# The lower part of the down weights moved from GpSimd to VectorE in two feed-forward stages

## What is computed

```
def _swiglu(h, w_gate, w_up, w_down):
    return (jax.nn.silu(h @ w_gate) * (h @ w_up)) @ w_down
...
g = lax.ragged_dot(xs, w_gate, group_sizes)
u = lax.ragged_dot(xs, w_up, group_sizes)
y = lax.ragged_dot(jax.nn.silu(g) * u, w_down, group_sizes)
```

## Time and profile before

| | |
|---|---|
| median of 3 runs | 4415.4 us (4410.6 to 4421.4) |
| the profiled execution | 4412.7 us, of which the span of the trace is 4410.9 us |
| TensorE matmul busy | 3861.9 us, 88% of the span |
| VectorE busy | 2323.4 us, 53% |
| ScalarE busy | 1755.2 us, 40% |
| GpSimd busy | 826.3 us, 19% |
| dense stage, about | 740 to 1520 us |
| expert stage, about | 1750 to 4380 us |

### The profile page before, as it was taken

The page is one execution under the profiler, slowest core; times in us unless marked ns, Lnnn a source line. Parts: engine busy times, 40 slices in busy tenths (PEclk is TensorE's granted clock), DMA queues, the critical chain, the costliest instruction groups (busy, mean ns, idle before and its releaser), DMA issues. The chain is left out here.

```text
span 4410.9 us, 65249 instructions
## 1 busy us (share of the span) xinstructions
PE 3861.9 (88%) x23414; PEld 3521.9 (80%) x23415; DVE 2323.4 (53%) x3372; ACT 1755.2 (40%) x2324; POOL 826.3 (19%) x319
## 2 busy tenths in 40 slices
PE   5998867999999762698999989988899998998993
PEld 3974445877877651688999989988899998998993
DVE  2338733454545452586654444448654487544555
ACT  5146613322322131555443333335533355443443
POOL 0000001111111121332222122213221233222222
PEclk8989878999999986899999999999999999999997
DMA  5136634323332233675553434346544366444554
GB/s 169 38 125 240 229 94 172 105 95 95 105 95 86 78 132 90 201 232 183 185 169 133 143 132 149 126 144 231 196 144 143 129 219 210 156 149 146 175 167 186
DMA packets 433192, 661.23 MB, mean 150 GB/s; under 512 B 33361, under 2 KB 348881, under 8 KB 432977
## 3 DMA queue, kind: packets, MB, share of 16 engines
q1 hardware_dynamic: 413026, 587.84, 40.0%
q0 software_dynamic: 15776, 55.61, 3.6%
q10 hardware_dynamic: 4176, 15.21, 0.9%
HBM read 599.32 MB, written 59.29 MB: 149 GB/s over the span
## 5 line engine op out<-in xcount | busy, mean ns | idle before, releaser
L1847 POOL TENSOR_TENSOR moe_d_lo<-moe_raw_d,moe_d_hi 128x2048 fp32r<-128x2048 f32 x126 | 582.8, 4625 | 1823.0 <-ACT moe_d_hi L1985 1823.0
L2153 DVE SCALAR_TENSOR_TENSOR moe_y_t<-moe_y,moe_cols,moe_y_t 128x256 f32<-128x256 f32 (+3 forms) x936 | 482.2, 534 | 185.5 <-PE moe_y L1898 176.9
L1896 PE MATMUL moe_g<-moe_x,moe_g_hi 128*128 128x352 f32 (+3 forms) x1344 | 421.2, 313 | 36.6 <-issue 36.3
L2100 DVE TENSOR_TENSOR moe_g_lo<-moe_raw_g,moe_g_hi 128x2048 fp32r<-128x2048 f32 x127 | 360.9, 2842 | 135.6 <-ACT moe_g_hi L1985 134.3
L1897 PE MATMUL moe_g<-moe_x,moe_g_hi 128*128 128x352 f32 (+3 forms) x1344 | 420.6, 313 | 0.0
L1896 PE MATMUL moe_y<-moe_h,moe_d_hi 128*128 128x352 f32 (+3 forms) x1344 | 417.9, 311 | 2.1 <-DVE moe_y_t L2153 1.1
L1898 PE MATMUL moe_g<-moe_x,moe_g_lo 128*128 128x352 f32 (+3 forms) x1344 | 419.2, 312 | 0.0
L1897 PE MATMUL moe_u<-moe_x,moe_u_hi 128*128 128x352 f32 (+3 forms) x1344 | 416.1, 310 | 0.0
L1897 PE MATMUL moe_y<-moe_h,moe_d_hi 128*128 128x352 f32 (+3 forms) x1344 | 416.0, 310 | 0.0
L1896 PE MATMUL moe_u<-moe_x,moe_u_hi 128*128 128x352 f32 (+3 forms) x1344 | 415.3, 309 | 0.0
L1898 PE MATMUL moe_u<-moe_x,moe_u_lo 128*128 128x352 f32 (+3 forms) x1344 | 415.0, 309 | 0.0
(11 more groups left out here) (317 smaller groups left out, 9504.4 us busy)
## 6 DMA issues: line engine op xcount, KB each, us to landing
moe_raw_g<-in_moe_w_gate SPq DMA_DIRECT2D x127, 1024.0 KB, 5.6
moe_raw_u<-in_moe_w_up SPq DMA_DIRECT2D x127, 1024.0 KB, 5.0
moe_raw_d<-in_moe_w_down SPq DMA_DIRECT2D x126, 1024.0 KB, 4.9
att_w_mod<-in_w_ada SPq DMA_DIRECT2D x20, 2048.0 KB, 8.5
scratch_y<-att_zeros SPq DMA_DIRECT2D x11, 2048.0 KB, 13.8
ffn_raw_g<-in_ffn_w_gate SPq DMA_DIRECT2D x22, 1024.0 KB, 5.4
ffn_raw_u<-in_ffn_w_up SPq DMA_DIRECT2D x22, 1024.0 KB, 5.4
ffn_raw_d<-in_ffn_w_down SPq DMA_DIRECT2D x22, 1024.0 KB, 4.8
```

The costliest lines, as they stand in the source:

```text
L1847: pool.tensor_tensor(d_lo[par][:, :, :], raw_d[:, :, :], d_hi[par][:, :, :].bitcast(F), ALU.subtract)\
L1896: pe.matmul(bank[:, 0:width], wh, moving[:, 0, 0:width], start=start, stop=False)
L2100: dve.tensor_tensor(lo[par][:, :, :], raw[:, :, :], hi[par][:, :, :].bitcast(F), ALU.subtract).then_inc(split, 1)
L2153: dve.scalar_tensor_tensor(y_t[:, db, 0:cols], y_ps[db % 4][:, 0:cols], gate, y_t[:, db, 0:cols], ALU.mult, ALU.add).then_inc(y_added, 1)
```

## The change

The subtraction that gives `d_lo` is taken off GpSimd's program and put into VectorE's step, after the add of block 4 (in a step without adds, after the rest of hidden f=1). The first increment of `d_split` moves with it. GpSimd keeps only the fetching of tokens.

```diff
         def _(pool):
             pool.sem_inc(x_turned, X0)
 
-            def rest_d(p, c, par):
-
-                n = p * C + c
-                pool.wait_ge(d_rounded, n + 1)
-                pool.tensor_tensor(d_lo[par][:, :, :], raw_d[:, :, :], d_hi[par][:, :, :].bitcast(F), ALU.subtract)\
-                    .then_inc(d_split, 1)
-
...
             def one_pass(p):
                 if has_next(p):
                     fetch(p + 1)
-                chunk_pairs(pool, p, 0, C - 1, lambda c, par: rest_d(p, c, par))
-
-            pool.sem_inc(d_split, W0)
+
...
             dve.sem_inc(u_split, W0)
+            dve.sem_inc(d_split, W0)
...
+            def rest_d(p, c, par):
+                rest(p * C + c, par, raw_d, d_hi, d_lo, d_rounded, d_split)
...
                     rest_hidden(p, c, par, 1, width)
                     if share:
-                        for db in range(2, KD):
+                        for db in range(2, 5):
+                            add(p, c - 1, db, cols, share == 1)
+                    rest_d(p, c, par)
+                    if share:
+                        for db in range(5, KD):
                             add(p, c - 1, db, cols, share == 1)
```

## The result

The changed kernel takes 4364.2 us (median of 4 runs, 4353.9 to 4366.6) against 4418.4 us for the kernel before (4410.6 to 4425.8, its runs beside these). The ratio is 0.9873, 95% interval 0.9849 to 0.9897. The forecast was 4370 us and faster. The profiled span fell from 4410.9 to 4364.8 us, by 46.1. The medians differ by 54 us: the profiled execution of the kernel before was one of its quicker ones.

A forecast was written before the change was run, and what follows sets the result against it. TensorE nearly full in wide passes; at width 128 it and VectorE wait for each other; GpSimd's subtraction blocks VectorE's. Forecast: 4412.7 - 23 (dense) - 10.6 (width 128) - 5.4 (starts) - 3.6 (ends) = 4370 us, range 4354 to 4400.

The forecast's parts named there:

- Dense stage: Dense steps: hidden subtraction no longer blocked, 20 TensorE waits of 1.16 us go, step 33.94 to 32.8 us; -23 us.
- Width 128: Two narrow expert passes: VectorE becomes the bound, step 13.66 to 13.22 us; -10.6 us over 24 steps.
- the 1.7 us wait for the first gate product: VectorE's wait in every other step of width 128, forecast to be filled, or nearly, by the new instruction.
- the floor of 13.1: Least step at width 128: VectorE's 10.86 us of work plus the new 2.20 us instruction.
- 0.15 for semaphores and low clock: Allowance in us put on the floor of a width 128 step, giving 13.22 us.
- Starts of narrow passes: First steps of three narrow passes: down subtraction fills VectorE's idle time, gate subtraction ends earlier; 3 x -1.8 = -5.4 us.
- Ends of narrow passes: Three narrow passes: TensorE's last wait for GpSimd and slow token splits shorten; 3 x -1.2 = -3.6 us.
- Width 160 and the wide passes: Expert passes where VectorE's added work is covered: 0 us for width 160, 0 for wide passes.
- (a): Rival: only the dense stage gives, narrow steps stay at 13.66 us, total 4389 us; 14%.
- (b): Rival: VectorE bounds the three narrow passes with idle time kept, width 128 step 15.2 us, total 4443; 6%.

The follow-up runs named there:

- pool_late: Kernel before, with GpSimd's down subtraction made to wait until VectorE has added block 4: 4402.9 us, ratio 0.9964.
- double_rest: Changed kernel with VectorE's down subtraction done twice, same output: 4467.6 us.
- early_place: Changed kernel, but VectorE's down subtraction stands ahead of the add of block 2 instead of behind block 4's: 4588.5 us, ratio 1.0377 to before.
- hidden_on_pool: Changed kernel, with the two short hidden subtractions of the narrow passes given to GpSimd: 4353.0 us, ratio 0.9837 to before.

## Why the prediction was right, point by point

**Dense stage, right.** -23 us forecast; the two passes are 11.8 us shorter each, -23.6. The chain (GpSimd blocks the hidden subtraction, the adds of blocks 2 to 7 stand behind it, TensorE waits for one of them) is shown at both ends: `pool_late` removes the blocking without moving the work and gets the same step. The step forecast was 32.8 us, measured 32.64: 1.30 us less a step, not 1.16.

**Width 128, right in kind, mis-sized.** VectorE became the bound, and the 1.7 us wait for the first gate product was filled. But a step is 12.79 us, not 13.22, and less than the floor of 13.1 I gave. The term that was off is VectorE's work: the 10.86 us of the earlier trace rows held waits that aren't work, 0.24 us ahead of the second gate half and 0.16 us of blocking in a subtraction that took 2.44 us instead of 2.28 (kernel before):

```profile
3063.66 2.44 DVE L2100 TENSOR_TENSOR moe_g_lo<-moe_raw_g,moe_g_hi 128x2048 fp32r<-128x2048 f32 x1
...
3067.15 0.42 DVE L2109 TENSOR_REDUCE moe_h_full<-moe_g 128x128 f32<-128x256 f32 x1 [0.24 <-PE moe_g L1895]
```

On top I added 0.15 for semaphores and low clock where none was due. Together that is 0.55 us, of which 0.43 showed. The blocking that went was also larger than I took it: the gate subtractions of steady steps in the kernel before average 3.2 us, 0.9 blocked a step and not 0.65. So the steady steps, 22 of them without the first two of each pass, gave -18.7 us instead of the -10.6 forecast for 24, nearly twice as much.

What is shown at this width is the end state: VectorE works without a pause (12.79 us), and a second instruction adds its whole length (`double_rest`). That the 1.7 us waits went because the blocking went, and with it TensorE's wait and its low clock, is the plain reading of the rows, but no run took the blocking away at width 128 without adding work to VectorE, so it stays argued.

**Starts of narrow passes, right.** Forecast -1.8 each. The first two steps together of such a pass became 1.5, 1.7 and 1.9 us shorter. The down subtraction does fill the wait for ScalarE; the gate subtraction behind it is 2.28 us long, where the earlier trace rows had 4.99:

```profile
2942.42 2.29 DVE L2092 TENSOR_TENSOR moe_d_lo<-moe_raw_d,moe_d_hi 128x2048 fp32r<-128x2048 f32 x1 [1.51 <-ACT moe_d_hi L1976]
...
2944.96 2.28 DVE L2092 TENSOR_TENSOR moe_g_lo<-moe_raw_g,moe_g_hi 128x2048 fp32r<-128x2048 f32 x1
```

**Ends of narrow passes, the cause right, the sum not to be seen.** TensorE's wait for GpSimd is one of 0.3 us for VectorE now, and two token splits take 1.28 us instead of 3.23 (kernel after, same pass):

```profile
PE moe_g L1874 <- DVE moe_d_lo L2092: 0.3, 1, 0.3
```
```profile
3112.30 1.28 DVE L2154 TENSOR_TENSOR moe_x<-moe_h_full,moe_x 128x512 fp32r<-128x512 f32 x2
```

But the gaps from such a pass to the next changed by -2.1, +1.7 and -2.0 us (-3.6 forecast in all, -2.4 measured), and gaps that the change can't reach moved by as much: those after wide passes by -1.0, -1.6, +1.0, +0.5 and +1.9.

**Width 160 and the wide passes, right.** 14.05 us before and after; its steps were just covered, as `double_rest` (+1.88 of 2.31) shows. In the wide passes the steps kept their length, but for 352, where a pass goes at 23.04 or at 23.20 us a step with no pattern that the kernels explain: before and after, one pass of three went at 23.04, but not the same one. That, and the first two steps of the pass of 256 and of the first of 352 (+0.9 and +2.2), came to +2.9 us over the stage.

**The sum.** -23.6 dense, -18.7 steady steps at 128, -5.1 starts, -2.4 ends, +2.9 wide passes, +0.8 all other gaps with the stretches ahead of the first rounding and behind the last: -46.1, against -42.7 forecast. The narrow steps gave 8.1 us more than forecast, and ends, wide passes and gaps 4.9 less. That the total came so near is in part luck: its terms are worse than their sum.

**The rivals.** (a) is out: expert steps gave their share alone (0.9932). (b), VectorE full with its idle time kept, did not come, but `early_place` is its mechanism made real: three adds earlier in VectorE's order and a step of width 128 costs 17.08 us, more than the 15.2 of (b). What kept it away is the place after block 4, and 6% was a chance for that place alone. The Trainium skill's advice ("Perfetto Trace Analysis", section "Optimizing Scalar/DVE Operations"), that a saturated DVE may hand work to GpSimd, is borne out in a small form only. With the 4.6 us instruction on GpSimd a step of width 128 took 13.63 us, with it on VectorE 12.79, so against the whole change the advice would have spoken wrongly; with two instructions of 0.46 us, in `hidden_on_pool`, it gave 0.44 us a step.

## What to carry to other kernels

An engine that is idle most of the time isn't free to use: look which instructions of its neighbour start while it runs, and what is queued behind them. Before moving work off it, try to move its moment; in the stage where TensorE is the bound that gave the whole gain. Where the work goes to an engine that becomes the bound, its place in that engine's order can decide more than its length: here doing the instruction twice cost 2.36 us a step, and doing it three adds earlier cost 4.3. Put it behind the last thing that another engine waits for in that round, and ahead of a wait.

## What the runs showed of the hardware

- While GpSimd runs an elementwise instruction that reads SBUF, a VectorE instruction with both inputs in SBUF doesn't get slower, it waits for GpSimd's end and then takes its usual time (4.93, 3.99, 2.84, 1.35 us instead of 0.68 or 2.28), whatever the tiles. An instruction with one operand in PSUM isn't touched (0.75 us beside GpSimd's 4.61). It works the other way round too: GpSimd took 2.34 us instead of 0.46, and 3.16 instead of 1.04, when VectorE began first, the latter by 0.02 us. The Trainium skill says the same ("SBUF — State Buffer", section "SBUF: two separate sides"): whichever starts first holds the shared ports for its whole instruction, and the other is fully blocked. These rows agree, and it held with no tile in common.
- A wait of 3.2 us in each step cost more than itself: TensorE's granted clock was 0.76 in the 7 us behind it and 0.90 over such steps (`early_place`), 1.00 in the same steps with waits of at most 1.1 us (kernel after), and 0.92 over a pass with waits of 1.9 us in every other step, 0.88 in such a step (kernel before). With waits of up to 3.4 us it was 0.91 in `double_rest`, and there it cost nothing, as VectorE was the bound.
- The stretch ahead of the dense stage, which is the same in all these kernels, ended anywhere from 784.6 to 799.0 us. Terms of a few us in such a sum can be read from step lengths, but not from totals. The dense step and the wide ones up to 320 repeated to 0.01 us; steps of width 128 with GpSimd at work lay at 13.63 and 13.69 in two kernels with the same expert stage, those of width 160 at 14.05 to 14.15, and those of width 352 at one of two values.
